# A kernel of two transformer blocks in float32: fourteen modulation tiles of the second layer stand in another stage

## What is computed

```python
for layer in range(DEPTH):
    mod_l = jnp.split((jax.nn.silu(c) @ w_mod[layer] + b_mod[layer])[:, None, :], 6, axis=-1)
    mod_c = jnp.split((jax.nn.silu(c_ctx) @ w_mod[layer] + b_mod[layer])[None, None, :], 6, axis=-1)
    hl = modulate(rmsnorm(xl, norm_g[layer, 0]), mod_l[0], mod_l[1])
    ...
    yc, yl = even_mixer(hc, hl, ...) if layer % 2 == 0 else rwkv_mixer(hc, hl, ...)
    xl = xl + mod_l[2] * rmsnorm(yl, norm_g[layer, 1])
    hl = modulate(rmsnorm(xl, norm_g[layer, 2]), mod_l[3], mod_l[4])
    xl = xl + mod_l[5] * rmsnorm(conv_ffn(hl, ...), norm_g[layer, 3])
```

## Time and profile before

| | |
|---|---|
| runs | 2857.36, 2863.51, 2868.78 us |
| the profiled execution | 2867.41 us, of which the span of the trace is 2865.6 us |
| TensorE busy | 2681.2 us (94%) |
| VectorE, ScalarE, GpSimd busy | 1760.4 (61%), 1347.1 (47%), 109.4 us (4%) |
| mean granted TensorE clock | 0.974 |
| loaded from HBM | 343.49 MB, 120 GB/s over the span |
| recurrences of the fifth mixer | about 1366 to 1504 us |
| gate products of feed-forward 4 | about 1587 to 1856 us |
| its down products | from 1862 us |

### The profile page before, as it was taken

How to read it: one execution, slowest core, us unless ns; L and a number is a source line. 1 busy time by engine, 2 the same in 40 slices (tenths; PEclk the granted TensorE clock), 3 DMA queues, 4 the chain that set the end, 5 groups by cost and what they waited for, 6 DMA issues and landing times.

```text
span 2865.6 us, 58680 instructions
## 1 busy us (share of the span) xinstructions
PE 2681.2 (94%) x24308; PEld 2195.1 (77%) x24308; DVE 1760.4 (61%) x2716; ACT 1347.1 (47%) x2152; POOL 109.4 (4%) x152
## 2 busy tenths in 40 slices
PE   8999999999999999999888999999998888888998
PEld 7887788888877888877666877777676776775986
DVE  6756557578465676423566777745675554565885
ACT  6645656466455665423343522334444444432333
POOL 0000000000000000000000000000001222220000
PEclk9999999999999999999898999999999999998999
DMA  6554435455544455344001333331120000003442
GB/s 258 186 190 165 162 133 191 177 191 184 184 158 148 156 191 176 148 184 154 2 2 41 131 147 147 132 110 58 74 94 2 4 4 25 4 4 119 169 152 105
DMA packets 49960, 348.32 MB, mean 122 GB/s; under 512 B 5536, under 2 KB 5536, under 8 KB 9504
## 3 DMA queue, kind: packets, MB, share of 16 engines
q1 hardware_dynamic: 49248, 342.45, 33.3%
q0 software_dynamic: 448, 2.11, 0.2%
HBM read 343.49 MB, written 1.05 MB: 120 GB/s over the span
## 4 chain that ended last, share of the span: by engine, by line
PE 78%; DVE 13%; ACT 4%; issue 3%; DMA 1%; DVEq 0%; ACTq 0%; POOL 0%; SPq 0%
PE psum L170 76%; DVE arena L98 3%; DVE ring_low L87 2%; PE psum L175 2%; DVE arena L87 2%; DVE wide L87 1%; ACT w_high L144 1%; DVE ring L87 1%; ACT wide L138 1%; DMA ring<-in_evt 1%; ACT arena L144 1%; ACT arena L140 0%; DVE wide L98 0%; DVE small L106 0%; DVE arena L94 0%
## 5 line engine op out<-in xcount | busy, mean ns | idle before, releaser
L170 PE MATMUL psum<-x_both,w_high 128*128 128x512 f32 (+1 forms) x2800 | 842.0, 372 | 9.4 <-DVE arena L87 7.8
L87 DVE TENSOR_TENSOR ring_low<-ring,w_high 128x2048 fp32r<-128x2048 f32 (+2 forms) x252 | 559.8, 2221 | 415.1 <-ACT w_high L144 400.4
L144 ACT ACTIVATE w_high<-ring 128x2048 fp32r<-128x2048 f32 (+2 forms) x252 | 469.1, 1861 | 517.6 <-PE psum L170 236.0
L170 PE MATMUL psum<-x_both,ring_low 128*128 128x256 f32 (+1 forms) x2104 | 603.1, 300 | 0.0
L170 PEld LDWEIGHTS psum<-x_both,w_high 128*128 128x128 f32 x2800 | 492.4, 188 | 105.8 <-issue 18.4
L170 PE MATMUL psum<-w_high,x_both 128*128 128x512 f32 (+1 forms) x1376 | 435.1, 393 | 10.3 <-issue 9.7
L170 PEld LDWEIGHTS psum<-x_both,ring_low 128*128 128x128 f32 x2104 | 397.0, 189 | 32.2 <-DVE x_both L98 0.9
L170 PEld LDWEIGHTS psum<-w_high,x_both 128*128 128x128 f32 x1376 | 261.1, 191 | 73.1 <-issue 19.9
L170 PE MATMUL psum<-ring_low,x_both 128*128 128x512 f32 (+1 forms) x688 | 267.6, 389 | 0.0
L144 ACT ACTIVATE arena<-psum 128x256 f32<-128x256 f32 (+1 forms) x341 | 148.4, 435 | 204.0 <-PE psum L170 176.8
L98 DVE SCALAR_TENSOR_TENSOR arena<-arena,prm 128x256 f32<-128x256 f32 x396 | 192.1, 485 | 14.2
(11 more groups left out here) (224 smaller groups left out, 3419.6 us busy)
## 6 DMA issues: line engine op xcount, KB each, us to landing
ring<-in_f_gu SPq DMA_DIRECT2D x88, 1024.0 KB, 4.8
ring<-in_w_mod SPq DMA_DIRECT2D x48, 1024.0 KB, 4.9
ring<-in_fu SPq DMA_DIRECT2D x44, 1024.0 KB, 4.9
ring<-in_f_dn SPq DMA_DIRECT2D x40, 1024.0 KB, 4.8
ring<-in_w_in SPq DMA_DIRECT2D x28, 1024.0 KB, 4.7
ring<-in_fd SPq DMA_DIRECT2D x20, 1024.0 KB, 4.9
ring<-in_rkvr SPq DMA_DIRECT2D x12, 1024.0 KB, 4.9
ring<-in_w_out SPq DMA_DIRECT2D x8, 1024.0 KB, 4.8
```

Of the source, the lines that this page charges most:

```text
L87: self.done(self.eng.tensor_tensor(o, a, b, op), then)
L144: self.done(self.eng.activation(o, i, ACT.Copy, scale=scale), then)
L170: ins = self.eng.matmul(o, l, r, start=a, stop=z)
```

## The change

The 14 tiles n = 4 to 10 of the second layer leave the gate products of feed-forward 4. In the plan they stand between the last token weights (evt) and the output weights (evo) of the fifth mixer, held to slots 2 and 3. In the recurrences, TensorE multiplies the two tiles of n = 4 + j at the end of phase 2 of each j below 7, into bank 5, ScalarE copies them there at the end of its phase 2, and in phase 3 TensorE turns them and VectorE adds the bias. The operand `spad` and the copied rows lie in slot 4 of the ring, so the first gate tile, which gets that slot, waits for the last turn. The first down tile of feed-forward 4 is held to slot 0.

```diff
--- before.py
+++ after.py
@@ -187,12 +187,6 @@
 
 
 
-def mod_parts(f):
-
-
-    return (4 + f // 3, f % 3) if f < 21 else (None, 3)
-
-
 EVO = ((0, 1), (0, 0), (1, 0), (1, 1))
 
 
@@ -206,9 +200,6 @@
     def ffn_tiles(i, gu, dn, mod=None):
         for f in range(22):
             plan.append((("gu", i, f), gu[f], WS))
-            n, part = mod_parts(f)
-            if mod is not None and part < 2:
-                mod_tile(mod, 2 * n + part)
         for n in range(2):
             for g in range(6):
                 w = 512 * min(4, 22 - 4 * g)
@@ -236,6 +227,8 @@
         for g in range(2):
             plan.append((("evt", n, g), dr["evt"][n, g], WS))
             mod_tile(1, 2 * n + g)
+    for m in range(8, 22):
+        mod_tile(1, m)
     for n, g in EVO:
         plan.append((("evo", n, g), dr["evo"][n, g], WS))
     ffn_tiles(4, dr["fu"][0], dr["fd"][0], 1)
@@ -255,7 +248,8 @@
 
 
 APART = {"ra1": 512, "ra2": 1024, "rw1": 1024, "rg1": 1024}
-HELD_OUT = {("evo", 0, 1): 0, ("rw2",): 3, ("rg2",): 3, ("rwo", 0, 0): 4}
+HELD_OUT = {("evo", 0, 1): 0, ("dn", 4, 0, 0): 0, ("rw2",): 3, ("rg2",): 3, ("rwo", 0, 0): 4}
+HELD_OUT.update({("mod", 1, n, g): 2 + g for n in range(4, 11) for g in range(2)})
 HELD_OUT.update({("rkv", 1, j): i for j, i in enumerate((4, 0, 1, 4))})
 HELD_OUT.update({("rkv", 0, j): i for j, i in enumerate((0, 1, 4, 0))})
 HELD_OUT.update({("rkv", 2, j): i for j, i in enumerate((1, 2, 0, 1))})
@@ -769,8 +763,6 @@
                         if k == 7 and cols == LAT:
                             then = w_free(key) if half else gate_mm((4, f))
                         half_products(T, k, cols, b, (high(key), low(key)), 1024 * half + 128 * k, then)
-                    if k == 7 and cols == LAT:
-                        mod_pe(T, 1, 4, f)
 
             norm_pe(T, CONV[0], range(4))
             for k in range(8):
@@ -913,12 +905,6 @@
                 gate_up(1, range(4, 8))
             for f in range(2 if late or i == 4 else 0, 22):
                 gate_up(f, range(8))
-                if i == 4:
-                    n, part = mod_parts(f)
-                    if part < 2:
-                        mod_pe(T, 1, n, part)
-                    elif part == 2:
-                        mod_turn_pe(T, 1, n)
             tbs = range(tok // 128)
             for n in range(2):
                 for g, blocks_here in down_steps(i, n, tbs):
@@ -1017,8 +1003,6 @@
                     high_part(A, i, f - 1)
                 if i != 5 and (i, f) != (4, 21):
                     split_on(split_act, A, ("gu", i, f))
-                if i == 4 and mod_parts(f)[1] == 1:
-                    mod_act(A, 1, mod_parts(f)[0])
                 if i == 4 and f == 21:
                     conv_gelu(A, i, 21)
             if i == 5:
@@ -1180,8 +1164,6 @@
             if i < 4:
                 halves_dve(D, i)
             for f in range(22 if i >= 4 else 0):
-                if i == 4 and f and mod_parts(f - 1)[1] == 2:
-                    mod_dve(D, 1, mod_parts(f - 1)[0])
                 conv_taps(D, i, f)
                 if f:
                     conv_product(D, i, f - 1)
@@ -1298,19 +1280,19 @@
         out_mm = signal("out_mm", [(l, n) for l in TWO for n in TWO])
         MODS = [(l, n) for l in TWO for n in range(12)]
         mr_ok, mt_mm, mod_ok = [signal(n, MODS) for n in ("mr_ok", "mt_mm", "mod_ok")]
-        spad_ok = signal("spad_ok", [("m", 0), ("m", 1), "e", "c"])
+        spad_ok = signal("spad_ok", [("m", 0), ("m", 1), "e", "s", "c"])
         pick = small[:, 212:214]
 
         def spare_of(l, n):
 
             if l == 0 and n < 8:
                 return ("m", n // 4), MY[:, 3712:3968], MY[:, 3968:4480]
-            even = l == 0 or n < 4
-            x = Y8[:, 0, :] if even else CPROD.rearrange("p a t -> p (a t)")
-            return "e" if even else "c", x[:, 512:768], x[:, 0:512]
+            place = "e" if l == 0 or n < 4 else "s" if n < 11 else "c"
+            x = {"e": Y8[:, 0, :], "s": ring[:, 4, :], "c": CPROD.rearrange("p a t -> p (a t)")}[place]
+            return place, x[:, 512:768], x[:, 0:512]
 
         def mod_bank(l, n):
-            return 7 if n < (8, 4)[l] else 7 - n % 2
+            return 7 if n < (8, 4)[l] else 5 if l and n < 11 else 7 - n % 2
 
         def mod_pe(T, l, n, g):
             place, spad, _ = spare_of(l, n)
@@ -2249,6 +2231,11 @@
                 if (j, ph) == (7, 3):
                     for n in FOUR:
                         mlstm_scores(T, 7, n)
+                if j < 7 and ph == 2:
+                    for g in TWO:
+                        mod_pe(T, 1, 4 + j, g)
+                if j < 7 and ph == 3:
+                    mod_turn_pe(T, 1, 4 + j)
                 if j and ph == 3:
                     mlstm_values(T, j - 1)
                 yield
@@ -2293,6 +2280,8 @@
                         col = 16 * z + 4 * kb + hd
                         A.act(MPT[z][:, kb, 128 * kb:128 * kb + 128], ED[:, 128 * kb:128 * kb + 128], ACT.Exp,
                               ml_a(("diag", j)) if kb == kbs[3] else None, bias=gc[:, col:col + 1])
+                if j < 7 and ph == 2:
+                    mod_act(A, 1, 4 + j)
                 if (j, ph) == (7, 2):
                     A.act(small[:, 216:217], ident[:, 0:1], ACT.Sqrt)
                 if j % 2 and ph == 3:
@@ -2370,6 +2359,8 @@
                     for n in FOUR:
                         mlstm_weights(D, 7, n)
                     gla_sums(D, 3)
+                if j < 7 and ph == 3:
+                    mod_dve(D, 1, 4 + j)
                 if j and ph == 3:
                     mlstm_factors(D, j - 1)
                     if j % 2 == 0:
@@ -2824,6 +2815,7 @@
                 ve.wait_ge(*lsn_a[i])
                 D.stt(x, x, 0.0, a, ALU.min, ALU.subtract, lsn_ok(i))
             ve.wait_ge(*w_free["evt", 3, 1])
+            mod_vectors(D, 1, 4)
             both(gla_dve(D), mlstm_dve(D))
             rows_in_dve(D)
             for g in (1, 0):
@@ -2835,7 +2827,7 @@
             gate_mult(D, ("e", 0), 0)
             D.fill(IMG, 0.0)
             D.fill(IMC, 0.0, cleared(4))
-            mod_vectors(D, 1, 4)
+            mod_vectors(D, 1, 11)
             ve.wait_ge(*eo_mm[1, 1])
             D.copy(YO[:, 1, 512:1024], bank(5), eo_d((1, 1)))
             gate_factors(D, ("e", 1))
@@ -3968,6 +3960,8 @@
                     eng.wait_ge(*w_free[slot_before[key]])
                 if key == ("ra1",):
                     eng.wait_ge(*xt_mm[RAW[0], 7])
+                if key == ("gu", 4, 0):
+                    eng.wait_ge(*mt_mm[1, 10])
                 if key in AFTER_SCAN:
                     for g in TWO:
                         eng.wait_ge(*sc_mm[g][15, "y"])
```

## The result

The kernel with the change takes 2881.93 us (median of 7 runs, 2875.11 to 2885.72), the kernel before 2862.06 us in the same comparison (7 runs, 2854.27 to 2868.78): ratio 1.0064, 95% interval 1.0047 to 1.0082. That is 19.9 us slower. The forecast was 2884 us, 20.5 us slower, and the rivals of "no change" and "faster" are out.

A forecast was written before the change was run, and what follows sets the result against it. TensorE, 94% busy, was taken to bound the kernel. Terms -20.9 + 18 + 23.4 = +20.5 us on the profiled 2867.4 gave 2887.9, less 3.9 for the median: 2884 us, range 2867 to 2898.

The forecast's parts named there:

- no change: Whole kernel: the time stays within 0.5% (14.3 us) of the kernel before; chance 0.20.
- faster: Whole kernel: the change makes it faster, only by way of (d), -18.9 us, 2845 us; chance 0.03.
- Part 1: Gate products of the fifth feed-forward: removing 14 tiles at 1.09 us and 7 turns at 0.81 us saves 20.9 us.
- Part 2: Recurrences of the fifth mixer: 19.2 us of added tiles and turns, less 2 absorbed, plus 1 for slow clock: +18 us.
- The one wait that was named as absorbing: Recurrences: 1.92 us before the product at 1485.63, where VectorE has a backlog; such waits take about 2 us in all.
- Part 3: After the gate products: late first down tile delays the first down product from T + 6.6 to T + 30.0, +23.4 us.
- The zero terms: Recurrences and around: ScalarE and VectorE copies and additions, shared bank 5, hidden loads and zeroed stationary cost nothing.
- (a): Recurrences: the tiles hide in TensorE's idle time, +4.5 us in all, 2868 us; chance 0.11.
- (b): Recurrences: denser work lifts the clock and brings back at most 15 us, +5.5 in all, 2869 us; chance 0.04.
- (c): After the gate products: the hole does not grow, -2.9 us in all, 2861 us; chance 0.05.
- (d): Both (a) and (c): tiles hide and the hole does not grow, -18.9 us, 2845 us; chance 0.03.
- (e): Recurrences: the tiles push them into half clock, 36 us instead of 18, 2902 us; chance 0.07.

The follow-up runs named there:

- experiment 3: Experiment 1 without the fourteen modulation tiles, their loads, turns, copies and additions (vectors filled with zeros): 2835.87 us, ratio 0.9907 to the kernel before.
- experiment 1: Changed kernel with the first down tile in a slot that comes free earlier, so its load is early again: 2852.48 us, ratio 0.9975 to the kernel before.
- experiment 2: Changed kernel, load still late, but ScalarE and VectorE split down tiles 0 and 1 behind the first hidden values: 2859.46 us, ratio 0.9988 to the kernel before.
- experiment 5: The changed kernel itself, unaltered, timed again on the same chip as experiment 6: 2877.11 us, ratio 1.0060 to the kernel before.
- experiment 6: Experiment 1 timed a second time, unaltered, beside experiment 5: 2854.12 us, ratio 0.9974 to the kernel before.
- experiment 4: Experiment 1 with the pair of tiles of j = 1 issued ahead of the transposes that wait for VectorE: 2852.25 us, ratio 0.9965 to the kernel before.
- experiment 7: Experiment 1's kernel with the last of seven tile pairs moved from the recurrences behind the last gate product: 2847.69 us, ratio 0.9953 to the kernel before.

## Why the prediction was right

**Part 1, gate products: -20.9 forecast, -23.6 measured.** The mechanism is right, TensorE never waits there (245.11 busy of 245.15), and the term was mis-sized by 2.7 us. (The 243 us in the prediction are a window that begins 26 us into the stage; the whole stage went from 268.69 to 245.13.) The sum took the gap between products near a tile as the undisturbed pace. In TensorE's timeline after the change, where no tile is near, 48 products lie between these two starts, 0.227 us each:

```profile
1660.42 0.39 PE L170 MATMUL psum<-x_both,ring_low 128*128 128x512 f32 x1
...
1671.30 0.39 PE L170 MATMUL psum<-x_both,ring_low 128*128 128x512 f32 x1
```

The 47 gaps behind a tile that the prediction used took 10.79 us instead of 47 x 0.2267 = 10.65, and 0.10 of these 0.14 us lie in the first two gaps behind the tile (1640.45 to 1641.01, 0.56 us where two gaps elsewhere take 0.46). The whole period of the kernel before, from behind one tile to behind the next, ends here:

```profile
1652.55 0.73 PE L170 MATMUL psum<-x_both,w_high 128*128 128x512 f32 x2
```

It took 1652.55 - 1640.45 = 12.10 us with the same 48 products and one tile, so a tile costs 12.10 - 10.88 = 1.22 us, and by the next period, which has a turn (to 1664.39, 11.84 us), a turn costs 0.96. Each is some 0.14 us more than the gap around it shows: 21 x 0.14 = 2.9, and 20.9 + 2.9 = 23.8. In a stream that never waits, a tile is priced by the length of a whole period with it and without it.

**Part 2, recurrences: +18 forecast, +17.5 measured** (+17.6 over all readings). The total is right and two of its terms are not. The step that waits on TensorE's own previous products absorb nothing is confirmed in the changed kernel: VectorE's waits at the transposes total 8.5 us where they were 8.2.

```profile
PE psum L175 <- DVE wide L87: 8.5, 3, 3.1
...
PE psum L170 <- ACT arena L138: 0.8, 1, 0.8
```

The one wait that was named as absorbing, 1.92 us before the product at 1485.63, is now 0.8. But it absorbed nothing either, because in experiment 3, without any tile, it is as short:

```profile
1488.20 1.98 PE L170 MATMUL psum<-arena 128*128 128x512 f32 x4 [0.75 <-ACT arena L138]
```

What the tiles did absorb were other short waits, 1.5 us of the 2 assumed, and the wait of 1.7 us in the run of 64 products, for which the prediction has no term, took that back. The other adjustment, +1 for tiles that fall in half clock, had the wrong sign: four of the seven pairs do take 2.34, 2.87, 2.67 and 3.64 us instead of 1.92, 3.8 us more in all, but the recurrences as a whole were granted 0.91 instead of 0.89, so that the stage grew by 1.6 us less than the 19.2 of full-clock work. An absorption of 2 us that in sum did not happen and a clock that gave where it was to take cancel, and that the total came out within 0.5 us is luck.

**Part 3, the hole: +23.4 forecast, +23.2 measured,** step by step: issued at the end of the gate products, landed after 4.83 (forecast 5), ScalarE's half 1.92 behind it, VectorE's 2.30, the next low part done at 1871.82, T + 18.5 (forecast 18.7), then 11.27 (forecast 11.2). Experiments 1, 2 and 5 with 6 show that the late load is the cause, and that the order of ScalarE's and VectorE's lists makes 20.6 of the 23.2.

**The zero terms.** Hidden loads, the shared bank and the zeroed stationary cost nothing that the profile shows: the idle time in the recurrences is no longer than before, and from their end to the first gate product it is 82.51 us where it was 82.49.

**The rivals.** (a), that the tiles hide, is out: 16.4 us idle with them, 16.1 without. It was weighed with the advice of the Trainium skill (Perfetto Trace Analysis, Optimization Strategy) to interleave stretches with different bounds; here it paid where a tile stood ahead of a long wait (1.85 us in experiment 4, the whole pair in experiment 7), and where the tiles of the change stand it paid 1.5 us of 19.2. (b), a clock lifted by denser work, brought 0.89 to 0.91, some 2 us and no 15. (c) and (d) are out by the hole. (e) is out as well. The Trainium skill (TensorE: Matmul & The Clock Gate, Why this matters for your kernels) asks for no idle gaps between bursts of products, and the trace agrees that a gap is followed by slow ones, in both kernels alike. The first start 0.43 us apart (1883.65 to 1884.08 above), where 0.23 is the full pace, and the first 4.1 us behind the hole are granted 0.54, mostly the 1.2 GHz level, in the kernel before (hole 6.63) as after the change (29.84). The first ten gaps between products take 4.11 us before, 4.09 after and 3.73 in experiment 1 (hole 6.61). So the longer hole costs its length and no more.

**Of the whole:** the three parts were right to 3 us each and the sum, +20.5, is 0.6 from the difference of the medians. The second timing of the changed kernel gave +15.9, so the closeness of that 0.6 is luck.

## What to carry to other kernels

When a load plan is edited, follow each remaining tile to its new slot, ask whose use now frees it, and what stands behind the instruction that consumes it on each in-order engine: here the move of the tiles alone won 7 to 9 us, and the late load of one down tile cost 23. Work moved into a stage with idle time is free only ahead of a wait whose releaser doesn't depend on the products behind it; compare the idle time with and without, wait by wait, because equal sums can hide waits that went and one that came. And compare stages, not spans, because a clock that scatters in code far away can be as large as the effect.

## What the runs showed of the hardware

The recurrences, the same instructions each time and with many waits, are granted a clock between 0.90 and 0.93 from one execution to the next and take 153.4 to 157.7 us with an idle time that stays the same; in the window from 2200 to 2560 us it lies between 0.95 and 0.99. The gate products, which never wait, took 245.12 or 245.13 us in each of seven executions. The products behind a tile of another shape lose 0.14 us more than the gap in their starts shows, most of it in the first two; what in TensorE does this wasn't tried. And TensorE can stand 1.7 us in the middle of a run of equal products for which the profile shows no releaser: in six profiles of six that have this wait, a 16 KB packet of the instruction queue had ended 1.38 to 1.45 us before TensorE went on.
